# One 2 MB load of expert weights is issued ahead of a wait for the sorted token rows

## The chip, the cores and the metric

The kernel runs on one core of a Trainium2 chip. The metric is the device time of one execution in microseconds (us). PE is TensorE, DVE is VectorE, ACT is ScalarE, POOL is GpSimd, SP is SyncE; SP computes nothing and issues nearly all transfers between HBM and on-chip memory.

## The reference

Three layers over 512 tokens of width 1024. The first is a hybrid layer (latent attention and an RWKV-7 scan) that ends in a mixture of 32 experts; two layers with three mixing branches and a dense feed-forward follow. The change lies in the mixture of experts:

```python
expert_ids = gsel[:, None] * EXPERTS_PER_GROUP + top_idx      # two experts for each token
...
for e in range(N_EXPERTS):
    hidden = jax.nn.silu(t @ w_gate[e]) * (t @ w_up[e])       # 1024 -> 256
    y = y + combine[:, e:e + 1] * (hidden @ w_down[e])        # 256 -> 1024
```

Each expert has a gate and an up matrix (1 MB each in fp32) and a down matrix (1 MB).

## The kernel before

The program is one instruction stream per engine, written out by hand; the engines meet at semaphores. Its sections are A (the first layer's mixing and the routing), M (the experts), B (the last experts' results) and L (the other two layers). SP's stream is in `sp_all`, PE's share of section M in `pe_M`.

**Sorting.** Each token goes to two experts, and each expert has 64 row places. POOL writes the normalized rows of the tokens to their places in the HBM tensor `sorted_x` (in `pool_all`): first eight small indirect transfers of weights to `sorted_w` (L1575), then eight indirect transfers of 128 rows of 4 KB each (L1582, 512 KB each), which raise the semaphore `sorted`. These go through DMA queue q0; everything that SP issues goes through q1, and what ACT issues through q10.

**Pairs.** Section M handles the experts two at a time: 16 pairs, p = 0 to 15. For each pair PE does in this order:

- the gate and up products `gu{p}` (L1461, 32 matmuls). They need the pair's rows, already turned, and its gate and up weights, 4 MB in two transfers (x = 0 and 1, one expert each);
- the turning of the next pair's rows, `xt{0,1}_{p}` (`turn_rows`, L699, 8 transposes). They need the next pair's 128 rows in on-chip memory (`rows_in1`, `rows_in0`);
- the turning of the hidden values (L1474), the down products `md{0,1}_{p}` (L1493, 16 matmuls), and the products that put the pair before back into token order (L1441, L1442).

PE takes its instructions strictly in this order. Pair 0 needs no sorted row from HBM: its rows come from matmuls with a placement matrix (`px0`, `px1`, L687). The rows of pairs 1 and 2 are loaded from `sorted_x` by the loop over b (L2542), those of the later pairs by L2551.

**Weights.** `fill_gates(j, p)` (L2494) issues the two gate and up transfers of pair p into buffer j = p % 2, 2048 KB each. That buffer is free when `gu{p-2}` is done. One transfer is left out there: the first half of pair 2's gate weights goes to the idle `ring` instead (L2536). So `fill_gates(0, 2)` issues one transfer, the second half. `fill_down(p)` (L2500) issues the down weights, 1024 KB for each x, and `fill_down(1)` only one of them. Both are waited for on PE by `gates_full` and `down_full`.

SP goes through its list in order: a wait holds up all that stands behind it, and its transfers share one queue.

Of the kernel before, what the change touches and what calls it, by code (L numbers as in the profile page):

```python
# [21 lines left out]
P = 128  # L22
T = 512
NT = T // P
# [188 lines left out]
def build(nc, ts_, out):  # L213
# [40 lines left out]
    with ExitStack() as ctx:  # L254
# [3 lines left out]
        def sem(name):  # L258
            return ctx.enter_context(nc.semaphore(name))
# [27 lines left out]
        sorted_x = nc.dram_tensor("sorted_x", [ROWS + 2 * T, D], F32, kind="Internal").ap()  # L287
# [17 lines left out]
        def ev(name):  # L305
            if name not in events:
                events[name] = sem(name)
            return events[name]
# [995 lines left out]
        XG = [arena[:, 12800:12800 + D], arena[:, 15872:15872 + D]]  # L1304
# [1173 lines left out]
        def sp_all(sp):  # L2478
            e = sp.e
# [10 lines left out]
            def fill_gates(j, at_):  # L2490

                for x in range(2):
                    if (at_, x) != (2, 0):
                        e.dma_start(GATE_SLOTS[j][:, 4 * x:4 * x + 4, :], expert_slots(at_, 6 * x, 4)).then_inc(gates_full[j][x], 16)  # L2494

            def fill_down(at_):

                for x in range(2):
                    if (at_, x) != (1, 0):
                        e.dma_start(DOWN[:, 2 * x:2 * x + 2, :], expert_slots(at_, 6 * x + 4, 2)).then_inc(down_full[x], 16)  # L2500

            def expert_slots(at_, s, n):
                if isinstance(at_, int):
                    at_ = at0["M"] + at_ * RM + s
                    return stream[at_:at_ + n].rearrange("a p n -> p a n")
                return stream[bass.ds(at_ * RM + (at0["M"] + s), n)].rearrange("a p n -> p a n")
# [29 lines left out]
            e.dma_start(ring[:, 0:4, :], expert_slots(2, 0, 4)).then_inc(ev("ring_gates"), 16)  # L2536
            e.wait_ge(ev("weights_sorted"), 16 * 2 * NT)
            e.dma_start(ROW_WEIGHT, sorted_w[0:ROWS, :].rearrange("(n p) w -> p (n w)", p=P), allow_slow_non_contiguous=True).then_inc(ev("weights_in"), 16)
            e.wait_ge(ev("sorted"), 16 * 2 * NT)
            sp.e.wait_ge(*sp.filled("px1"))  # L2540
            for b in (1, 2):
                e.dma_start(XG[b % 2], sorted_x[b * P:(b + 1) * P, :]).then_inc(ev(f"rows_in{b % 2}"), 16)  # L2542
            sp.sec = "M"
            for p in range(NPAIR - 1):
                j = p % 2
                sp.e.wait_ge(*sp.filled(f"gu{p}"))
                if p < NPAIR - 2:
                    fill_gates(j, p + 2)
                if p < NPAIR - 3:
                    sp.e.wait_ge(*sp.filled(f"xt1_{p}"))  # L2550
                    e.dma_start(XG[1 - j], sorted_x[(p + 3) * P:(p + 4) * P, :]).then_inc(ev(f"rows_in{1 - j}"), 16)  # L2551
                sp.e.wait_ge(*sp.filled(f"md1_{p}"))
                fill_down(p + 1)
# [25 lines left out]
        @block.sync  # L2579
        def _(eng):  # L2580
            sp = Engine(eng, "sp")
            sp_all(sp)
# [210 lines left out]
```

## Time and profile before

| | |
|---|---|
| median of 3 runs | 2498.12 us (2497.9 to 2500.25) |
| the profiled execution | 2503.14 us, of which the span is 2501.3 us |
| PE busy | 2349.0 us (94%) |
| DVE busy | 1236.5 us (49%) |
| ACT busy | 748.0 us (30%) |
| POOL busy | 646.4 us (26%) |
| q1, SP's transfers | 278.51 MB |
| q0, POOL's transfers | 4.20 MB |
| chain that ended last | PE 78%, DVE 9%, DMA 7%, issue 3% |

The span is the time between the first and the last instruction of the profiled execution. Times inside it are counted from its start. The chain that ended last is followed back from the last instruction, at each step to what released it; its shares say where the time went. The digits of the page's slices are tenths: 9 is 90% busy or more.

### The profile page before, as it was taken

How to read it: one execution, taken by the hardware profiler on the slowest of the kernel's cores; microseconds unless marked ns; L12 is line 12 of the kernel's file. 1: busy time of each engine (PE TensorE's matmuls, PEld its weight loads, DVE VectorE, ACT ScalarE, POOL GpSimd, SP SyncE). 2: the span in 40 equal slices, each digit the busy share in tenths (PEclk: the TensorE clock that was granted, in tenths of full speed). 3: DMA queues.
4: the chain of work that ended last, by engine and by line, in shares of the span. 5: the costliest groups of instructions: out<-in, count | busy, mean ns of one | idle time of the engine just before them, and what ended most of it. 6: DMA issues, size and time to landing. Idle time of an engine off the chain costs nothing.

```text
span 2501.3 us, 30836 instructions
## 1 busy us (share of the span) xinstructions
PE 2349.0 (94%) x12552; PEld 1666.0 (67%) x12552; DVE 1236.5 (49%) x2171; ACT 748.0 (30%) x1176; POOL 646.4 (26%) x288
## 2 busy tenths in 40 slices
PE   6999778888899979999999999999999999999999
PEld 2334455563444448767878888888766887888887
DVE  2355555543365550585355677411177436666710
ACT  2333412212111123543233333223344323333321
POOL 0000000001000014223444444444322444444443
PEclk9999888879999989999999999999999999999999
DMA  5331000005899933212333333222211333333322
GB/s 200 109 93 34 30 2 2 2 5 227 335 409 409 402 126 110 68 51 77 96 97 94 94 100 94 92 93 104 86 60 51 100 94 93 96 98 96 98 76 101
DMA packets 79250, 287.79 MB, mean 115 GB/s; under 512 B 9187, under 2 KB 9571, under 8 KB 78598
## 3 DMA queue, kind: packets, MB, share of 16 engines
q1 hardware_dynamic: 75718, 278.51, 32.6%
q0 software_dynamic: 1408, 4.20, 0.4%
q10 hardware_dynamic: 1984, 3.10, 0.4%
q8 instruction: 101, 1.65, 0.3%
q14 instruction: 39, 0.32, 0.0%
HBM read 278.11 MB, written 16.07 MB: 118 GB/s over the span
## 4 chain that ended last, share of the span: by engine, by line
PE 78%; DVE 9%; DMA 7%; issue 3%; ACT 2%; POOL 1%; SPq 0%; ACTq 0%; DVEq 0%; another core or an unknown queue 0%; POOLq 0%
PE bank L1863 12%; PE bank L1865 12%; PE bank L1864 12%; DMA arena<-in_stream 6%; PE bank L530 5%; DVE arena L389 3%; PE bank L2012 3%; PE bank L2013 3%; PE bank L2011 3%; PE bank L1493 2%; PE bank L850 2%; PE bank L1848 2%; PE bank L1850 2%; PE bank L1849 2%; DVE arena L395 2%
## 5 line engine op out<-in xcount | busy, mean ns | idle before, releaser
L1594 POOL TENSOR_TENSOR ring_low<-ring,W_high 128x1024 fp32r<-128x1024 f32 x252 | 606.2, 2405 | 1135.4 <-ACT W_high L399 1135.4
L1863 PE MATMUL bank<-H_high,W_high 128*128 128x512 f32 x1408 | 555.4, 394 | 7.9 <-ACT arena L399 5.9
L1865 PE MATMUL bank<-H_high,ring_low 128*128 128x512 f32 x1408 | 548.4, 390 | 0.0
L1864 PE MATMUL bank<-H_low,W_high 128*128 128x512 f32 x1408 | 548.1, 389 | 0.0
L399 ACT ACTIVATE W_high<-ring 128x1024 fp32r<-128x1024 f32 x264 | 279.8, 1060 | 874.1 <-PE bank L1865 552.2
L1863 PEld LDWEIGHTS bank<-H_high,W_high 128*128 128x128 f32 x1408 | 264.2, 188 | 78.2 <-issue 23.2
L1864 PEld LDWEIGHTS bank<-H_low,W_high 128*128 128x128 f32 x1408 | 264.4, 188 | 55.8 <-issue 1.9
L1865 PEld LDWEIGHTS bank<-H_high,ring_low 128*128 128x128 f32 x1408 | 264.3, 188 | 55.6
L389 DVE TENSOR_TENSOR arena<-bank,root 128x512 f32<-128x512 f32 x116 | 79.7, 688 | 306.7 <-PE bank L1865 306.5
L399 ACT ACTIVATE arena<-bank 128x512 f32<-128x512 f32 (+5 forms) x179 | 77.0, 441 | 337.3 <-PE bank L825 118.0
L395 DVE SCALAR_TENSOR_TENSOR arena<-arena 128x512 f32<-128x512 f32 (+3 forms) x63 | 117.8, 1871 | 99.4 <-ACT arena L403 98.7
L1575 POOL DMA_INDIRECT sorted_w<-arena x8 | 7.8, 980 | 614.9 <-DVE arena L395 612.8
L389 DVE TENSOR_TENSOR arena<-arena 128x512 f32<-128x512 f32 (+5 forms) x180 | 146.8, 820 | 15.1 <-ACT arena L403 11.8
L2012 PE MATMUL bank<-arena_split,W_high 128*128 128x512 f32 x352 | 138.7, 394 | 0.0
L2011 PE MATMUL bank<-arena_split,W_high 128*128 128x512 f32 x352 | 137.5, 391 | 0.1
L2013 PE MATMUL bank<-arena_split,ring_low 128*128 128x512 f32 x352 | 137.5, 391 | 0.0
L530 PE MATMUL bank<-H,ring 128*128 128x512 f32 (+1 forms) x288 | 132.8, 606 | 2.3 <-DVE H L395 2.3
L395 DVE SCALAR_TENSOR_TENSOR arena<-arena,bank 64x64 f32<-64x64 f32 (+2 forms) x112 | 52.8, 474 | 165.3 <-ACT arena L403 101.1
L403 ACT ACTIVATE arena<-arena 128x512 f32<-128x512 f32 (+3 forms) x182 | 109.9, 620 | 72.8 <-DVE arena L1079 37.8
L395 DVE SCALAR_TENSOR_TENSOR X<-bank,X 128x512 f32<-128x512 f32 x32 | 22.1, 692 | 218.8 <-PE bank L2013 204.2
L395 DVE SCALAR_TENSOR_TENSOR arena<-arena,p 128x512 f32<-128x512 f32 x104 | 103.3, 993 | 40.8 <-ACT arena L403 39.0
L1461 PE MATMUL bank<-arena,early 128*64 128x512 f32 x496 | 113.0, 592 | 1.1 <-issue 1.1
(260 smaller groups left out, 3259.9 us busy)
## 6 DMA issues: line engine op xcount, KB each, us to landing
ring<-in_stream SPq DMA_DIRECT2D x289, 512.0 KB, 3.6
arena<-in_stream SPq DMA_DIRECT2D x31, 2048.0 KB, 12.8
arena<-in_stream SPq DMA_DIRECT2D x31, 1024.0 KB, 10.5
sorted_x<-in_zero_row SPq DMA_DIRECT2D x4, 2048.0 KB
arena<-sorted_x SPq DMA_DIRECT2D x15, 512.0 KB, 16.3
X<-in_x SPq DMA_DIRECT2D x1, 2048.0 KB, 9.0
ring<-in_stream SPq DMA_DIRECT2D x1, 2048.0 KB, 7.7
out<-X SPq DMA_DIRECT2D x8, 256.0 KB, 6.9
```

The source lines that it names most:

```text
L389: return V.tensor_tensor(o, a, b, op)
L395: return V.scalar_tensor_tensor(out=o, in0=a, scalar=s, in1=b, op0=op0, op1=op1)
L399: return S.activation(o, i, f)
L530: i = mm(o, w[:, k, 0:32] if m == 3 else w[:, k, :], H[:, k, :], start=k == 0, stop=k == KD - 1)
L1461: i = mm(o, XF[:, c, 64 * x:64 * x + 64], w, start=c == 0, stop=c == KD - 1)
L1594: return G.tensor_tensor(ring_low[:, slot, :], ring[:, slot, :], W_high[:, s % 2, :].bitcast(F32), ALU.subtract)
L1863: mm(ps[:, :], wh[:, k, :], H_high[:, k, :], start=k == 0, stop=False)
L1864: mm(ps[:, :], wh[:, k, :], H_low[:, k, :], start=False, stop=False)
L1865: i = mm(ps[:, :], wl[:, k, :], H_high[:, k, :], start=False, stop=k == KD - 1)
L2011: mm(ps[:, :], wh[:, t_ % TPS, :], high, start=k == 0, stop=False)
L2012: mm(ps[:, :], wh[:, t_ % TPS, :], low, start=False, stop=False)
L2013: i = mm(ps[:, :], wl[:, t_ % TPS, :], high, start=False, stop=k == KF - 1)
```

## The change

The loads of the rows of pairs 1 and 2, with the wait for `sorted` ahead of them, move into the first turn of the pair loop, behind `fill_gates(0, 2)`.

```diff
             e.wait_ge(ev("weights_sorted"), 16 * 2 * NT)
             e.dma_start(ROW_WEIGHT, sorted_w[0:ROWS, :].rearrange("(n p) w -> p (n w)", p=P), allow_slow_non_contiguous=True).then_inc(ev("weights_in"), 16)
-            e.wait_ge(ev("sorted"), 16 * 2 * NT)
             sp.e.wait_ge(*sp.filled("px1"))
-            for b in (1, 2):
-                e.dma_start(XG[b % 2], sorted_x[b * P:(b + 1) * P, :]).then_inc(ev(f"rows_in{b % 2}"), 16)
             sp.sec = "M"
             for p in range(NPAIR - 1):
                 j = p % 2
                 sp.e.wait_ge(*sp.filled(f"gu{p}"))
                 if p < NPAIR - 2:
                     fill_gates(j, p + 2)
+                if p == 0:
+                    e.wait_ge(ev("sorted"), 16 * 2 * NT)
+                    for b in (1, 2):
+                        e.dma_start(XG[b % 2], sorted_x[b * P:(b + 1) * P, :]).then_inc(ev(f"rows_in{b % 2}"), 16)
                 if p < NPAIR - 3:
                     sp.e.wait_ge(*sp.filled(f"xt1_{p}"))
```

On SP, between the last load of section A and the first turns of the pair loop, the difference is the following. L2536 is the first half of pair 2's gate weights, L2538 the weights of the sorted rows, L2494 a gate transfer (4x1024 elements on 128 partitions), `arena<-sorted_x` the rows of a pair, L2500 a down transfer. `bank_full0` is the semaphore of `px1` and of `gu0`.

```order
 L2536 DMA ring<-in_stream 128x4x1024 [waits bank_full2]
 L2538 DMA small<-sorted_w 128x16x1 [waits weights_sorted]
-L2542 DMA arena<-sorted_x 128x1024 [waits bank_full0,sorted]
-L2542 DMA arena<-sorted_x 128x1024
 L2494 DMA arena<-in_stream 128x4x1024 [waits bank_full0]
-L2551 DMA arena<-sorted_x 128x1024 [waits bank_full5]
+L2549 DMA arena<-sorted_x 128x1024 [waits sorted]
+L2549 DMA arena<-sorted_x 128x1024
+L2552 DMA arena<-sorted_x 128x1024 [waits bank_full5]
 L2500 DMA arena<-in_stream 128x2x1024 [waits bank_full0]
 L2494 DMA arena<-in_stream 128x4x1024 [waits bank_full1]
```

The two row loads moved behind one gate transfer; L2551 only has a new line number. No other engine's list differs except in line numbers.

## Rows read from the trace of the kernel before

**Rows 1.** The page: the span, and the DMA engines' busy tenths in 40 slices.
```profile
span 2501.3 us, 30836 instructions
...
DMA  5331000005899933212333333222211333333322
```

**Rows 2.** Timeline of SP, 605 to 720 us: start, length, line, operation.
```profile
624.38 0.37 SPq L2538 DMA_DIRECT2D small<-sorted_w  x1
637.27 0.81 SPq L2542 DMA_DIRECT2D arena<-sorted_x  x2
638.12 0.43 SPq L2494 DMA_DIRECT2D arena<-in_stream  x1
...
649.71 0.38 SPq L2500 DMA_DIRECT2D arena<-in_stream  x1
656.58 0.93 SPq L2494 DMA_DIRECT2D arena<-in_stream  x2
```

**Rows 3.** SP's own waits, 590 to 680 us: total, times, longest.
```profile
SPq L2542 <- DMA sorted_x<-arena: 12.4, 1, 12.4
```

**Rows 4.** Timeline of POOL: the first and the last of eight row scatters.
```profile
623.48 0.96 POOL L1582 DMA_INDIRECT sorted_x<-arena  x1 [0.31 <-issue]
...
632.29 0.95 POOL L1582 DMA_INDIRECT sorted_x<-arena  x1 [0.30 <-issue]
```

**Rows 5.** Timeline of PE, 610 to 705 us; in brackets the idle time before, and what ended it.
```profile
624.63 7.09 PE L1461 MATMUL bank<-arena,early 128*64 128x512 f32 x32 [1.10 <-issue]
...
641.24 1.97 PE L699 MATMUL bank<-cst,arena 128*128 128x128 f32 x8 [5.28 <-DMA arena<-sorted_x]
...
644.20 5.48 PE L1493 MATMUL bank<-arena 128*64 128x512 f32 x16 [0.56 <-ACT arena L399]
649.50 7.05 PE L1461 MATMUL bank<-arena,early 128*64 128x512 f32 x32
...
677.27 3.65 PE L1493 MATMUL bank<-arena 128*64 128x512 f32 x16
...
693.90 3.65 PE L1493 MATMUL bank<-arena 128*64 128x512 f32 x16 [0.95 <-DMA arena<-in_stream]
```

**Rows 6.** PE's waits from 660 to 880 us, the rest of section M.
```profile
PE bank L1493 <- DMA arena<-in_stream: 12.0, 12, 1.3
```

**Rows 7.** Busy time by stretch; PEclk is the granted clock, then DMA share, GB/s.
```profile
633.00:636.00 3.00, 1.37 (x10) 1.01 (x8) 0.00 (x0) 0.29 (x2) 0.24 (x1) 1.00 1.00 392
...
638.00:640.00 2.00, 0.00 (x0) 0.00 (x0) 0.00 (x0) 0.00 (x0) 0.00 (x0) 0.50 0.70 182
...
643.00:648.00 5.00, 4.43 (x13) 1.61 (x14) 3.21 (x6) 0.38 (x1) 0.00 (x0) 0.51 1.02 410
648.00:651.00 3.00, 3.00 (x16) 1.08 (x14) 1.34 (x2) 1.19 (x2) 0.00 (x0) 1.00 0.09 15
...
654.00:657.00 3.00, 3.00 (x17) 1.14 (x14) 0.00 (x0) 0.38 (x1) 0.00 (x0) 1.00 0.01 3
...
659.00:690.00 31.00, 31.00 (x148) 14.23 (x147) 18.57 (x33) 3.68 (x9) 0.00 (x0) 1.00 1.02 409
```

**Rows 8.** Issue to landing of the two row loads at L2542: min/median/max.
```profile
DMA to landing us min/median/max: 3.9/4.4/4.8
```

**Rows 9.** Issue to landing of L2494's three transfers between 630 and 660 us.
```profile
DMA to landing us min/median/max: 8.0/9.4/13.6
```

**Rows 10.** Timeline of ACT: the first operation on `gu0` and on `gu1`.
```profile
635.71 0.38 ACT L403 ACTIVATE arena<-bank 128x256 f32<-128x256 f32 x1 [10.79 <-remote]
...
656.59 0.38 ACT L403 ACTIVATE arena<-bank 128x256 f32<-128x256 f32 x1 [6.27 <-PE bank L1461]
```

**Rows 11.** DMA queues, 633 to 638 us: packets, MB, share of 16 engines.
```profile
q0 software_dynamic: 381, 1.36, 69.5%
```

**Rows 12.** DMA queues, 627 to 628 us.
```profile
q1 hardware_dynamic: 1217, 0.00, 68.4%
q0 software_dynamic: 63, 0.26, 62.6%
```

## Prediction

> **What bounds the kernel now.** I began with the page. The kernel spans 2501.3 us, and its DMA row has one stretch of nines, the slices from about 625 us on [rows 1]: the experts' weights. So I read that stretch engine by engine, SP first, since the change is only in SP's list.
>
> SP issues the load of the rows' weights at 624.38, then nothing until 637.27, when it loads the rows of pairs 1 and 2; right behind, at 638.12, comes pair 2's gate transfer [rows 2]. SP's own waits name the cause: 12.4 us for the scatter into `sorted_x` [rows 3]. POOL issues eight of these scatters between 623.48 and 632.29 [rows 4], and they keep the DMA engines full (share 1.00, 392 GB/s from 633 to 636 [rows 7]).
>
> Who needs what SP holds back? PE finishes `gu0` about 631.7 (624.63 + 7.09) and then idles until the rows of pair 1 are there: its transposes start at 641.24 after a wait for that very load [rows 5]. The rows were issued at 637.27 and took 3.9 us [rows 8], which is the 641.2. So the path is scatter, row load, transposes, and then PE in unbroken order: down products at 644.20, `gu1` at 649.50 [rows 5]. The end of `gu1` releases SP at 656.58 [rows 2] for pair 3's gate weights. From 659 on the DMA engines are full (share 1.02, 409 GB/s [rows 7]), and PE waits for down weights 12 times, 12.0 us in all, the first time at 693.90 [rows 5, 6]. The later pairs are therefore bound by a train of transfers whose first car leaves when `gu1` is done.
>
> **What the change does.** It adds no instruction and no byte. It moves two row loads behind one gate transfer of 2048 KB, 2.10 MB, on the same queue. There are two sides to cost.
>
> *The gate transfer comes earlier: worth nothing.* Its weights are wanted by `gu2`, which starts around 665 and shows no wait on it; PE's only waits after 660 are for down weights [rows 6]. Nor does it relieve the train. After it the queue runs dry: the DMA share is 0.09 from 648 to 651 and 0.01 from 654 to 657 [rows 7], so the train starts when `gu1` ends, not when the wires come free. The one down transfer between them is issued at 649.71 [rows 2], when PE is done with its buffer. The cover of this zero is those two dry stretches.
>
> *The rows come later: all of it on the path.* Two moments are unknown to the trace, since in it SP is held until 637.27: when SP would see `gu0`, and how q0 and q1 share the engines.
>
> The gate transfer's bytes need 2.10 MB / 409 GB/s = 5.1 us, a row load's 0.52 MB 1.3 us [rows 7].
>
> Early signal: the last `gu0` matmul ends at 631.7 and SP issues there; by the lag of a transfer into an idle queue (issue 656.58, DMA full by 659) its bytes run from about 633. The scatter then has 1.36 MB left [rows 11], 3.4 us at 392 to 409 GB/s. If the two queues share evenly, the scatter's tail takes twice as long, `sorted` comes 3.4 us late, the gate transfer is done a little after it, while the row load starts up, and the rows land 3.4 us late. If q1 goes first, the scatter stands still for the whole 5.1 us and the rows land 5.1 us late. The nearest row for that choice is the microsecond from 627 on, where SP's load of row weights meets the scatter: 1217 packets of q1 against 63 of q0 [rows 12]. Those packets are tiny, so it is weak evidence, but an even turn for turn it is not.
>
> Late signal: ACT, which waits for the same semaphore as SP would, starts on `gu0` only at 635.71, 4 us after the matmuls' end, with no local releaser named, while on `gu1` it starts at 656.59, at once [rows 10]. If SP sees it at 635.7 too, the scatter is nearly through and undisturbed, and SP is free again for its row loads at 637.27. The rows now stand in one queue behind the gate transfer. A gate transfer into an empty queue lands 8.0 us after issue [rows 9], so at 643.7; one row load behind it adds 1.3: 645.0, or 3.8 us late. Counted by bytes alone (wires free at about 636.6, then 5.1 + 1.3 us, then some 0.8 us until the landing is seen, an estimate from the rows of before, whose bytes and landing stand that far apart) it is 643.8, or 2.6 us late.
>
> So the path gets longer by 2.6 to 5.1 us. I take 4.2, the middle of the early signal's 3.4 and 5.1, with the late signal's 3.8 close by: I can't tell which signal holds in a run without the profiler.
>
> The Trainium skill (page "DMA: Bandwidth & Descriptors", section "Queues, rings and completion order") says that an engine consumes one row's descriptors in ring order and takes turns between rows packet by packet. Even turns would give the 3.4 us; the trace's microsecond from 627 doesn't look even and leans to 5.1. The ring order is what makes the late signal cost anything, and the trace agrees in that pair 2's gate transfer, behind two row loads, landed after 9.4 us where one into an empty queue took 8.0.
>
> *The clock.* PE sat idle before 641.24, and the granted clock was 0.50 from 638 to 640 and still 0.51 on average from 643 to 648, full after it [rows 7]. That is 1.2 instead of 2.4 GHz. The down products of pair 0 took 5.48 us because of it, against 3.65 for pair 2's [rows 5]. With a longer idle PE restarts at half clock as before. If the clock returned later, the whole group would run at half clock, 7.3 us (+1.8); if earlier, 3.65 (-1.8). I take nothing and keep 1.8 either way for the range, though less than the whole of it is likely.
>
> *The sum.* Removed: SP's 12.4 us hold on the gate transfer, worth 0. Added: 4.2 us ahead of pair 0's transposes. Moved through: `gu1`, the start of the train, everything behind it, one to one, since PE has no slack between 641.24 and 656.6 and the train none after. The profiled execution of 2503.14 us would become 2507.3; on the median of the runs, 5.0 lower, 2498.12 + 4.2 = 2502.3 us.
>
> **Rivals.**
>
> *No change.* The rows overtake the gate transfer, or the gate transfer's bytes run in the gaps: between 638 and 640 the DMA share was only 0.70 at 182 GB/s [rows 7]. If the two loads shared the wires evenly instead of in order, the rows would need 2 x 1.3 us, some 1.3 us more: 2499.4 us. Against it: the scatter leaves no gap before 636 (1.00). A change of the order that does nothing at all would need a signal from `gu0` later than 637.27, and ACT had it at 635.71. Chance 0.12.
>
> *Faster.* The early gate transfer takes its bytes out of the busy train, which ends up to 5.1 us sooner while the rows are delayed less than that; 2495 us at best. It decides if the queue is not empty when pair 3's gates are issued at 656.58. It was empty (0.01 from 654), so 0.03.
>
> *Worse than forecast.* q1 goes first, and the clock comes back late too: 5.1 + 1.8 = 6.9, 2505.0 us. The idle of PE grows from 5.28 to over 10 us, which speaks for it; that a restart cost the same 1.2 GHz already speaks against. Chance 0.12. The forecast, 3 to 5.1 us, keeps 0.73.
>
> **How the numbers follow.** A measurement of this kernel tells 0.2%, 5.0 us, from no change. Faster by that is left 0.03. The forecast straddles the bound only at its top: q1-first with 5.1 us stands on it. I give 0.23 of the forecast's 0.73 to the far side, with the worse rival's 0.12 that makes slower 0.35; the other 0.50 and the no-change rival's 0.12 make 0.62 for within 0.2%. The range takes in the 2.6 of the byte count less part of the clock's 1.8, and the upper 6.9 with a microsecond for the spread of the runs (2.35 us): 2498.8 to 2506.2 us.
>
> **What the next profile would show.** SP issues the 2048 KB transfer first, at 631.8 (early) or 635.7 (late), and the row loads behind it. Early, q0's share falls below 1.00 after 633 and SP sees `sorted` at 640.7 or, with q1 first, 642.4; late, at 637.3 as before, and the row loads' landing time grows from 3.9 to about 7.7 us. PE's idle before the transposes grows from 5.28 to about 9.5 us, and pair 3's gates go out at about 660.8 instead of 656.58. The waits for down weights stay near 12 us. I am wrong if the transposes start by 642, if the train starts by 657, or if what is lost there comes back in the later pairs.

## The result, and the profile after

The changed kernel takes 2507.06 us, the median of 8 runs (2503.48 to 2509.62), against 2498.01 us for the kernel before in its 8 (2496.93 to 2501.81). The ratio is 1.0029, with a 95% interval of 1.0019 to 1.0039: slower by some 7 us, between 4.7 and 9.7. (The two medians lie 9.1 us apart; that too is inside the interval.) That is beyond 0.2%, so of my three classes "slower" (0.35) came true and not the likeliest, "within 0.2%" (0.62). On the median of 2498.12 us the ratio gives 2505.4 us; I had said 2502.3, in a range of 2498.8 to 2506.2.

The page after, its span and its DMA row:

```profile
span 2506.9 us, 30836 instructions
...
DMA  5431000005899933212233233222221333333322
```

The two spans differ by 5.6 us (2506.9 against the 2501.3 of [rows 1]), but executions also differ in when they reach the stage at issue. I therefore count from one instruction that both have, the start of pair 0's row transposes (L699 on `early`), and call it S. It lies at 621.70 us after, and at 622.47 us before.

SP's timeline after, 605 to 720 us:

```profile
623.72 0.37 SPq L2538 DMA_DIRECT2D small<-sorted_w  x1
631.04 0.37 SPq L2494 DMA_DIRECT2D arena<-in_stream  x1
641.41 0.81 SPq L2549 DMA_DIRECT2D arena<-sorted_x  x2
...
653.11 0.38 SPq L2500 DMA_DIRECT2D arena<-in_stream  x1
659.98 0.93 SPq L2494 DMA_DIRECT2D arena<-in_stream  x2
```

The gate transfer goes out at 631.04, and the wait for `sorted` behind it ends at 641.41. From SP's load of the row weights that is 17.7 us; before it was 12.9 (637.27 - 624.38) [rows 2]. The scatter ends 4.8 us later. PE's and ACT's timelines after:

```profile
621.70 1.06 PE L699 MATMUL bank<-cst,early 128*128 128x128 f32 x8 [0.73 <-issue]
...
645.45 1.97 PE L699 MATMUL bank<-cst,arena 128*128 128x128 f32 x8 [12.16 <-DMA arena<-sorted_x]
...
648.41 4.67 PE L1493 MATMUL bank<-arena 128*64 128x512 f32 x16 [0.56 <-ACT arena L399]
652.90 7.05 PE L1461 MATMUL bank<-arena,early 128*64 128x512 f32 x32
...
697.54 3.65 PE L1493 MATMUL bank<-arena 128*64 128x512 f32 x16 [0.96 <-DMA arena<-in_stream]
```

```profile
631.00 0.38 ACT L403 ACTIVATE arena<-bank 128x256 f32<-128x256 f32 x1 [6.85 <-PE bank L1461]
```

PE starts pair 1's transposes 23.75 us after S, against 18.77 before [rows 5]: 5.0 us later. Its down products took 4.67 us against 5.48, so 0.8 us comes back, and pair 3's gates leave 38.28 us after S against 34.11 (656.58 - 622.47) [rows 2]: 4.2 us later. PE's waits for down weights hardly change, 11.5 us from 662 to 900 us against 12.0 before:

```profile
PE bank L1493 <- DMA arena<-in_stream: 11.5, 13, 1.1
```

Where did the scatter's 4.8 us go? The DMA queues of the kernel after, first 633 to 636 us, then 636 to 641 us:

```profile
q0 software_dynamic: 141, 0.49, 55.7%
q1 hardware_dynamic: 70, 0.29, 37.8%
q10 hardware_dynamic: 27, 0.04, 5.5%
```

```profile
q1 hardware_dynamic: 347, 1.42, 70.6%
q0 software_dynamic: 176, 0.61, 30.1%
q10 hardware_dynamic: 21, 0.02, 1.4%
```

Between 633 and 641 q1 moved 1.71 MB of the gate transfer while the scatter moved 1.10 MB (0.49 + 0.61). Neither had the wires to itself: from 636 on q1 had 1.42 of 2.05 MB, seven tenths. And the wires moved less while the two met. The stretches 634 to 636 and 636 to 638 us, whose last three numbers are clock, DMA share and GB/s:

```profile
634.00:636.00 2.00, 0.00 (x0) 0.00 (x0) 0.00 (x0) 0.00 (x0) 0.00 (x0) 1.00 0.94 266
636.00:638.00 2.00, 0.00 (x0) 0.00 (x0) 0.00 (x0) 0.00 (x0) 0.00 (x0) 0.71 1.02 402
```

That is 266 GB/s at a share of 0.94, where the scatter alone moved 392 at 1.00 [rows 7]. The loss is short: from 636 on the two move 402 together, as much as either alone.

That explains 4.2 us. But the end of the span lies 1885.2 us after S (2506.9 - 621.7) and before it was 1878.8 (2501.3 - 622.47): 6.4 us. The other 2.2 us are lost much later. PE in the first of the two last layers, the kernel after:

```profile
1091.68 0.49 PE L1919 MATMUL bank<-arena 64*128 64x128 f32 x4 [1.04 <-ACT arena L399]
1093.00 0.47 PE L1863 MATMUL bank<-H_high,W_high 128*128 128x512 f32 x1 [0.83 <-DVE arena L2306]
```

These two short waits are in the kernel before as well, ending at 1090.22. Now the 10 us from 2 us ahead of the second wait's end, first before, then after (PE's busy time, then clock, DMA share, GB/s):

```profile
1088.22:1098.22 10.00, 8.49 (x41) 1.00 0.12 47
```

```profile
1091.00:1101.00 10.00, 8.49 (x32) 0.83 0.12 49
```

The same place in the program, the same busy time, but in the kernel after the granted clock averages 0.83: for about a third of the time PE had 1.2 instead of 2.4 GHz, and it did 32 matmuls where it had done 41. The same happens one layer on, near 1882 us, at the same instructions, in the kernel after alone (again PE's busy time, clock, DMA share, GB/s):

```profile
1882.00:1886.00 4.00, 3.70 (x10) 0.59 0.00 0
```

So the loss has two parts, 4.2 us ahead of the train of transfers, and two stretches of half clock far behind it, 1.4 us each by this account (2.8 in all, of which 0.6 is made up for by the shift shrinking from 4.2 to 3.6 us on its way to the first of them).

### The profile page after: what moved, and what is told of

It is laid out like the page before. It is cut to its first block, busy times and chain, and to the rows that moved or that the text cites. A ratio compares the mean times of both kernels' runs of the same rounds, so it can differ in the third digit from the quotient of the medians.

```text
span 2506.9 us, 30836 instructions
## 1 busy us (share of the span) xinstructions
PE 2349.7 (94%) x12552; PEld 1668.8 (67%) x12552; DVE 1237.6 (49%) x2171; ACT 748.1 (30%) x1176; POOL 646.4 (26%) x288
## 4 chain that ended last, share of the span: by engine, by line
PE 78%; DVE 9%; DMA 7%; issue 3%; ACT 2%; POOL 1%; SPq 0%; ACTq 0%; DVEq 0%; another core or an unknown queue 0%; POOLq 0%
PE bank L1863 12%; PE bank L1865 12%; PE bank L1864 12%; DMA arena<-in_stream 6%; PE bank L530 5%; PE bank L2012 3%; PE bank L2013 3%; PE bank L2011 3%; DVE arena L389 3%; PE bank L1493 2%; PE bank L850 2%; PE bank L1848 2%; PE bank L1850 2%; PE bank L1849 2%; DVE arena L395 2%
## 5 line engine op out<-in xcount | busy, mean ns | idle before, releaser
L395 DVE SCALAR_TENSOR_TENSOR arena<-arena 128x512 f32<-128x512 f32 (+3 forms) x63 | 117.9, 1871 | 99.3 <-ACT arena L403 98.7
L395 DVE SCALAR_TENSOR_TENSOR arena<-arena,bank 64x64 f32<-64x64 f32 (+2 forms) x112 | 52.8, 474 | 161.5 <-ACT arena L403 97.2
L395 DVE SCALAR_TENSOR_TENSOR X<-bank,X 128x512 f32<-128x512 f32 x32 | 22.1, 692 | 218.8 <-PE bank L2013 204.2
L395 DVE SCALAR_TENSOR_TENSOR arena<-arena,p 128x512 f32<-128x512 f32 x104 | 103.3, 994 | 40.8 <-ACT arena L403 39.0
```

Of the source, the lines that this page charges most:

```text
L395: return V.scalar_tensor_tensor(out=o, in0=a, scalar=s, in1=b, op0=op0, op1=op1)
```

## The experiments

All kernels compute the reference's output in full. Theory **T**: the gate transfer and the scatter's tail share the wires, so `sorted` comes late. **Q**: the rows are late because they stand behind the gate transfer in their queue. **C**: the rest is TensorE's clock, which falls or doesn't fall at those two gaps by the moment at which they come. **M**: the rest is lost within section M. The columns count from S, all from profiles: the start of pair 1's transposes, the issue of pair 3's gates, the end of PE's wait on L2306 (the gap), the end of the span; then the granted clock over 10 us around the gap.

| kernel | transposes | pair 3's gates | gap | end | clock | ratio |
|---|---|---|---|---|---|---|
| before | 18.77 | 34.11 | 467.75 | 1878.8 | 1.00 | |
| after | 23.75 | 38.28 | 471.30 | 1885.2 | 0.83 | 1.0029 |
| r0, after again | 24.12 | 38.48 | 471.58 | 1885.5 | 0.83 | 1.0025 [1.0016, 1.0034] |
| r1, half ahead | 22.07 | 37.46 | 471.03 | 1882.2 | 1.00 | 1.0018 [1.0009, 1.0027] |
| r2, behind the wait | 24.53 | 38.69 | 474.13 | 1885.2 | 1.00 | 1.0031 [1.0018, 1.0043] |
| r3, rows on ACT | 24.09 | 38.47 | 471.50 | 1885.3 | 0.83 | 1.0025 [1.0016, 1.0034] |
| r4, rows scattered first | 11.42 | 27.50 | 460.76 | 1871.9 | 1.00 | 0.9965 [0.9953, 0.9978] |
| r5, between the rows | 18.87 | 34.18 | 467.79 | 1878.8 | 1.00 | 0.9997 [0.9988, 1.0007] |
| r6, quarter | 20.35 | 34.92 | 468.00 | 1881.9 | 0.83 | 1.0013 [1.0003, 1.0022] |
| r7, before again | 18.98 | 34.20 | 467.79 | 1878.9 | 1.00 | 0.9999 [0.9989, 1.0008] |
| r8, 6 memsets | 18.37 | 32.22 | 467.48 | 1878.5 | 1.00 | one run |
| r9, 14 memsets | 18.60 | 34.03 | 467.74 | 1878.8 | 1.00 | one run |
| r10, 34 memsets | 18.63 | 33.98 | 470.72 | 1881.9 | 1.00 | one run |
| r11, 27 memsets | 18.98 | 34.18 | 470.06 | 1881.3 | 1.00 | one run |

**r0, the changed kernel again.**

> The changed kernel once more, unedited. The local measure in all these runs is the time from SP's load of the row weights (small<-sorted_w) to PE's first transpose of pair 1 (arena, after the wait on sorted_x): 16.86 us before, 21.73 us after. Theory T (the gate transfer's 2.10 MB and the tail of the scatter share the wires, so the signal sorted comes late): 21.7 us again, SP's row loads 4 to 5 us later than before. Theory C (whatever the change costs beyond about 4 us is the clock of TensorE, which falls for a short stretch in the last two layers when a 2 us gap of PE falls badly): runs at mean clock 0.969 take 2 to 3 us longer than runs at 0.971, and the profile has 0 to 3 such stretches after 1000 us, each worth about 1.3 us. Rival to C (the shift itself costs more later, in the experts' loop): all runs would be near 2507 whatever their clock. I expect 2502 to 2509 us, median near 2505.

Median 2507.32 us (2501.59 to 2509.41, 11 runs). The transposes came 22.17 us after SP's load of the row weights, close to the 21.7. The two stretches of half clock are there again. The runs whose mean clock was 0.969 took 4.5 us longer than those at 0.971 (2508.1 against 2503.6), more than the 2 to 3 expected. But mean clock doesn't tell the two stretches apart from what happens ahead of S: r3 has both at a mean of 0.971. Traces are kept of one execution of each kernel, so whether every run of the changed kernel has the stretches stays open.

**r1, half of the gate transfer ahead.** The other half goes behind the row loads, and PE's wait on `ring_gates` goes from 16 to 32 to match. On SP:

```diff
...
-                if p < NPAIR - 2:
-                    fill_gates(j, p + 2)
                 if p == 0:
+                    src = expert_slots(2, 6, 4)
+                    e.dma_start(GATE_SLOTS[0][:, 4:6, :], src[:, 0:2, :]).then_inc(ev("ring_gates"), 16)
                     e.wait_ge(ev("sorted"), 16 * 2 * NT)
...
+                    e.dma_start(GATE_SLOTS[0][:, 6:8, :], src[:, 2:4, :]).then_inc(gates_full[0][1], 16)
+                elif p < NPAIR - 2:
+                    fill_gates(j, p + 2)
```

> Half of the gate transfer (1024 KB) ahead of the wait for sorted, the other half behind the two row loads. T: 1.05 MB ahead of the scatter's tail, 2.6 us at 409 GB/s, so the local measure is 19.2 to 19.5 us and the time about 2500.5 us. Rival Q (what counts is that the rows stand behind the gate transfer in SP's queue): a half transfer issued at about 631 has landed long before sorted is up, so nothing stands ahead of the rows any more: 16.9 to 17.3 us, 2498 us.

Median 2505.02 us. SP's timeline:

```profile
621.35 0.37 SPq L2538 DMA_DIRECT2D small<-sorted_w  x1
628.76 0.37 SPq L2546 DMA_DIRECT2D arena<-in_stream  x1
637.86 0.81 SPq L2549 DMA_DIRECT2D arena<-sorted_x  x2
```

`sorted` is seen 16.5 us after the load of the row weights, 3.6 us later than the 12.9 before. The half transfer was issued 9.1 us ahead of the row loads. It landed 9.2 us after its issue, just as they went out, not long before as expected, but they weren't held up: the transposes began 3.6 us behind their issue, 3.9 before. So Q, which expected 16.9 to 17.3 us from the load of the row weights to the transposes, is refuted as the cause here: they came at 20.15. T expected 19.2 to 19.5, by bytes alone. Half the bytes cost 3.1 to 3.3 us (against r7 and before) and all of them 4.8 to 5.4, so the price doesn't go by the size of the transfer. An estimate from rows fits both: the bytes of q1 that ran before the scatter was through, 1.04 MB here and 1.71 in the changed kernel, take 2.5 and 4.2 us at 409 GB/s, and the low rate where the queues meet (256 GB/s over 2 us here, 266 there, instead of some 400) costs some 0.7 us more: 3.2 and 4.9.

**r2, the gate transfer behind the wait, ahead of the rows.**

```diff
+                if p == 0:
+                    e.wait_ge(ev("sorted"), 16 * 2 * NT)
                 if p < NPAIR - 2:
                     fill_gates(j, p + 2)
                 if p == 0:
-                    e.wait_ge(ev("sorted"), 16 * 2 * NT)
                     for b in (1, 2):
```

> The gate transfer behind the wait for sorted, but still ahead of the two row loads. It cannot touch the scatter. T alone: no delay of sorted, SP sees it as before; if only the wires of the scatter mattered, the local measure is 16.9 us and the time 2498 us. Q: the rows wait for 2.10 MB in their own queue, 5.1 us: 21.5 to 22 us, 2502 to 2503 us. I expect Q to hold here, since a queue in order has to cost the same bytes wherever they stand ahead of the rows.

Median 2508.26 us. Here the scatter is left alone, and the gate transfer can only stand in the queue. SP, then PE:

```profile
636.80 0.37 SPq L2494 DMA_DIRECT2D arena<-in_stream  x1
637.22 0.98 SPq L2550 DMA_DIRECT2D arena<-sorted_x  x2
```

```profile
646.12 1.97 PE L699 MATMUL bank<-cst,arena 128*128 128x128 f32 x8 [12.95 <-DMA arena<-sorted_x]
```

The rows take 8.9 us from issue to use instead of 3.9 [rows 8], 5.0 us more, close to the 5.1 of 2.10 MB at 409 GB/s. From the load of the row weights the transposes come at 22.6 us, above the 21.5 to 22 expected; the rest is SP's own 0.4 us for issuing the gate transfer and some 0.4 us by which `sorted` comes later than in the trace of before (13.3 against 12.9, but 13.25 in r7). So Q is a real mechanism, with about the price of its bytes. It just isn't the one at work in the changed kernel, where the rows' own loads took the usual time (641.41 to 645.45, 4.0 us).

**r3, the row loads on ACT's queue.** The two loads and their wait move from SP to ACT, behind its first operation on `gu0`.

```diff
+                if p == 0:
+                    e.wait_ge(ev("sorted"), 16 * 2 * NT)
+                    for b in (1, 2):
+                        e.dma_start(XG[b % 2], sorted_x[b * P:(b + 1) * P, :]).then_inc(ev(f"rows_in{b % 2}"), 16)
                 if p == NPAIR - 2:
                     e.dma_start(RELB[0:32, 0, 0:DH], ts_["rel_bias"]).then_inc(ev("rel_in"), 16)
...
-                if p == 0:
-                    e.wait_ge(ev("sorted"), 16 * 2 * NT)
-                    for b in (1, 2):
-                        e.dma_start(XG[b % 2], sorted_x[b * P:(b + 1) * P, :]).then_inc(ev(f"rows_in{b % 2}"), 16)
```

> The gate transfer goes ahead as in the changed kernel, but the two row loads (and their wait for sorted) go to ACT's queue, so nothing of SP's stands ahead of them. T: sorted is as late as in the changed kernel, 4 to 5 us, and the rows are hardly sooner: 21 to 21.7 us, 2502 to 2505 us. Q: the rows are free of the gate transfer, 16.9 to 17.5 us, 2498 us.

Median 2505.71 us. ACT's queue carries nothing of the gate transfer, and ACT sees `sorted` no sooner:

```profile
638.94 0.84 ACTq L1519 DMA_DIRECT2D arena<-sorted_x  x2
```

That is 18.4 us after the load of the row weights (620.53), and the transposes follow 3.7 us later. T holds: the lateness is in the scatter, whatever queue the rows take.

**r5, the gate transfer between the two row loads.** Against the kernel before:

```diff
-            for b in (1, 2):
+            for b in (1,):
                 e.dma_start(XG[b % 2], sorted_x[b * P:(b + 1) * P, :]).then_inc(ev(f"rows_in{b % 2}"), 16)
...
                     fill_gates(j, p + 2)
+                if p == 0:
+                    e.dma_start(XG[0], sorted_x[2 * P:3 * P, :]).then_inc(ev("rows_in0"), 16)
```

> The order before, except that the gate transfer goes between the row load of pair 1 and that of pair 2. Bytes ahead of pair 1's rows are what costs: none are ahead of them here, so PE's first transpose of pair 1 comes 16.9 us after SP's load of the row weights, as before, and the time is that of before (2498 to 2500 us). Rival: pair 2's rows, late by 5 us, hold up PE at the second turn; they are wanted at 656.5 and would be there by 650, so this should not be seen.

Median 2499.72 us, no difference. Pair 2's rows have the slack that pair 1's lack.

**r6, a quarter of the gate transfer behind the wait, ahead of the rows.** Against r1:

```diff
-                    e.dma_start(GATE_SLOTS[0][:, 4:6, :], src[:, 0:2, :]).then_inc(ev("ring_gates"), 16)
                     e.wait_ge(ev("sorted"), 16 * 2 * NT)
+                    e.dma_start(GATE_SLOTS[0][:, 4:5, :], src[:, 0:1, :]).then_inc(ev("ring_gates"), 16)
...
-                    e.dma_start(GATE_SLOTS[0][:, 6:8, :], src[:, 2:4, :]).then_inc(gates_full[0][1], 16)
+                    e.dma_start(GATE_SLOTS[0][:, 5:8, :], src[:, 1:4, :]).then_inc(gates_full[0][1], 16)
```

> Only a quarter of the gate transfer (512 KB) stands behind the wait for sorted and ahead of the row loads, the other 1536 KB behind them. With the queue in order the rows are late by the bytes ahead of them: 0.52 MB at 409 GB/s, 1.3 us, so 18.2 us after SP's load of the row weights (16.9 with none, 22.6 with 2.10 MB), and pair 3's gate weights go out 1 to 1.3 us later than before. Rival (a fixed price for any transfer ahead, about 3 us, as the half transfer cost 3.3 us where its bytes account for 2.6): 20 us. The time would be 2499 to 2500 or 2501 to 2502 us.

Median 2503.05 us. The transposes came 18.46 us after the load of the row weights, 1.4 to 1.6 us later than before (16.86, 17.03), as 0.52 MB should cost; there is no fixed price. Part of it came back at once through the clock: pair 3's gates are 0.7 to 0.8 us late and the gap only 0.2. Yet the end is 3.0 us late, because both stretches of half clock are there. That is why the time, expected at 2499 to 2500 us, came out higher.

**r7, the kernel before again.**

> The kernel before, unedited, for its own spread: 16.9 us for the local measure again, 2498 to 2500 us, ratio 1.000. If ACT starts on gu0 at once here (not 4 us after the matmuls, as in the trace of before), that late signal was a singular event of one execution.

Median 2499.64 us. All its columns agree with before to 0.2 us. ACT starts on `gu0` at once:

```profile
630.84 0.38 ACT L403 ACTIVATE arena<-bank 128x256 f32<-128x256 f32 x1 [6.84 <-PE bank L1461]
```

**r4, rows scattered ahead of the weights.** On POOL the eight blocks of rows go first; on SP the row loads go ahead of the load of the row weights.

```diff
-            po.e.wait_ge(*po.nth("weights", 1))
-            for n in range(2 * NT):
...
                     nc.gpsimd.indirect_dma_start(sorted_x, bass.IndirectOffsetOnAxis(ap=rows, axis=0), HT[:, i_, :], None).then_inc(ev("sorted"), 16)
+            po.e.wait_ge(*po.nth("weights", 1))
+            for n in range(2 * NT):
...
```

> The order before on SP for the gate transfer, but POOL scatters the eight blocks of rows ahead of the eight small blocks of weights, and SP waits for the rows first. If the scatter's end is what everything behind hangs on, the rows of pair 1 are in place before gu0 ends, and the next thing late is the row weights: POOL is done with them 20 us after its start as before, about 633, their load of some 3.6 us is in by 638.2, so the turning of the hidden values (L1474), at 643.0 before, starts near 638.8: 4.2 us earlier, 2494 us. Rival (the freed time is lost again): the train of weight transfers, which starts when gu1 is done, would have to start no earlier than 656.6; then 2498 us. If the clock of TensorE is what makes up the rest, the time differs from the shift at 656 by 0 to 3 us.

Median 2490.94 us (2490.2 to 2494.74, 6 runs), ratio 0.9965: it beats both kernels, by some 9 and 16 us (7.0 and 13.3 from S to the end in the profiles). POOL's first scatter and PE:

```profile
605.47 1.15 POOL L1578 DMA_INDIRECT sorted_x<-arena  x1 [605.01 <-DVE arena L389]
```

```profile
628.65 1.04 PE L699 MATMUL bank<-cst,arena 128*128 128x128 f32 x8
631.62 0.41 PE L1474 MATMUL bank<-cst,arena 128*128 128x128 f32 x2 [1.94 <-DVE arena L395]
```

The transposes wait for nothing now; what is late next is the row weights, whose load DVE's L395 waits for (3.64 us) and PE behind it (1.94 us). Pair 3's gates go out 6.6 to 6.7 us earlier, not 4.2, because the rows need only the row numbers, not the weights, and POOL could start that much sooner: 11.8 us ahead of S (617.23 - 605.47), where the first scatter of weights in r7 started 9.3 us ahead of it (at 612.30, S at 621.55).

**r8 to r11, a pure delay on DVE.** In front of the signal that opens the last two layers, n memsets of one column:

```diff
+            for _ in range(n):
+                V.memset(small[:, 59:60], 0.0).then_inc(dv.chained(), 1)
+                dv.e.wait_ge(dv.chain, dv.n)
             V.memset(small[:, 59:60], 0.0).then_inc(dv.tells("x_ready"), 1)
```

> The kernel before with a pure delay: six tiny memsets of one unused column, one behind the other on DVE, ahead of the signal that opens the two last layers; section M is untouched. Measured from the start of pair 0's row transposes to the end of the span, before took 1878.8 us in both of its profiles, the changed kernel 1885.2 and 1885.5, of which 4.2 and 4.4 are there when pair 3's gate weights go out. Theory C (the other 2.2 us are two short stretches of half clock, near 1092 and 1880 us, that come or go with the moment at which the same 2 us gap of PE falls, whatever moved it): a delay of some 0.8 us may bring both stretches, as a shift of 0.8 us in r6 did: 0.8 + 2.2 = 3.0, 1881.8 us, with the granted clock of 1080:1110 at 0.94; if it brings none, 1879.6. Rival M (the 2.2 us come from something that the changed order does in the experts' section): never more than the delay itself, 1879.6, and no new stretch.

> The same with fourteen memsets, about 1.8 us. C: the gaps fall elsewhere again; either 1880.6 us with no new stretch or 1882.8 with two. M: 1880.6.

> The same with thirty-four memsets, about 4.2 us, the shift of the changed kernel. C: with the shift of 4.2 us the two stretches come back as in the changed kernel: 1878.8 + 4.2 + 2.2 = 1885.2 us and 0.94 in 1080:1110. M: 1883.0 us, 1.00 in 1080:1110.

> Twenty-seven memsets, about 3.35 us on DVE. The three delays before showed that some 2.6 us of this delay is hidden (1.69 us of memsets: 1878.8 us from the start of pair 0's transposes to the end, as before; 4.20 us: 1881.85, with one more stretch of half clock between 880 and 945), so this one should move PE in the last two layers by 0.8 to 1.2 us, the shift that r6 had. C: the gaps near 1088 and 1877 then fall where they fell in r6, two stretches of half clock come, the granted clock of 1080:1110 is 0.94, and the time is 1878.8 + 1 + 2.2 = 1882 us. M (the 2.2 us belong to the order of the transfers in section M): 1.00 in 1080:1110, 1879.6 to 1880 us. If the shift comes out above 1.5 us, it tells nothing new.

These tests did not decide. On DVE the memsets took 0.69, 1.69, 4.20 and 3.31 us (r8, r9, r10, r11). They also weren't pure delays: in r8, r10 and r11 the clock from 880 to 945 us averaged 0.84, where before and r9 have 0.87, one more stretch of half clock ahead of the gap. In r8, which was 1.9 us early at pair 3's gates and 0.3 at the gap, it cost 1.6 us. If it cost the same in the others, some 2.6 to 2.8 us of the delay is hidden. r8 and r9 hardly moved the gap (0.3 us early and not at all). r10 and r11 moved it by 3.0 and 2.3 us and brought no stretch near it. C had forecast stretches for both (1885.2 and 1882 us), but for shifts of 4.2 and of 0.8 to 1.2 us that didn't come about, and r11's is above the 1.5 us named ahead of the run as telling nothing; M's 1883.0 for r10 failed as well. The shift of 0.2 to 0.3 or of 3.5 to 3.8 us, at which the stretches came elsewhere, was not met.

What the table shows on C, over all kernels: relative to before, the end is as late as the gap, to 0.1 us, in every kernel whose clock there is 1.00 (among them r1 3.3 and 3.3; r10 3.0 and 3.0; r11 2.3 and 2.4; r4 -7.0 and -7.0). In the four with 0.83 the end is 2.7 to 2.8 us later than the gap: after (3.55 and 6.4), r0 (3.83 and 6.6), r3 (3.75 and 6.5), r6 (0.25 and 3.0). r2's gap was 6.4 us late, and so was its end; of those, 4.6 were there at pair 3's gates, and in the stretch 880 to 945 us its mean clock was 0.84 where before had 0.87, as in r8: it too lost to the clock, at another place. So M is refuted for after, r0, r3 and r6 (in the changed kernel 3.9 us are left at the end of section M, fewer than the 4.2 at pair 3's gates): what they lost beyond the gap they lost behind section M, at half clock. That the moment of the gap decides is what the table suggests (0.04 and 3.28 without, 0.25 and 3.55 with a stretch). So does the moment of the fall: in after, r0 and r3 it lies at 472.5 to 472.6 us behind S, though the gap ends anywhere from 471.30 to 471.58, and in r6 at 469.2, with the gap at 468.00. In each of the four it is 1.0 to 1.2 us behind the gap. None of this was forced by an experiment, so it stays an inference.

## Why the prediction was right in its direction and too small

**What bounds the stage.** Right: the path is scatter, row load, transposes, and all behind them. r4 is the strongest evidence: with the rows' scatter and row loads first in their queues, the kernel gained 7.0 us from S to the end. None of the three signs that the prediction named for being wrong came up: the transposes didn't start by 642, nor the train by 657, and little came back in the later pairs: at the last issue of down weights (L2500 at 867.63, before at 864.53) 3.9 of the 4.2 us are left.

**The earlier gate transfer is worth nothing.** Right. The wires are dry again ahead of the train (0 GB/s from 658 to 660, pair 3's gates at 659.98), and PE's waits for down weights stay at 11.5 to 11.8 us in every kernel with a changed place of the transfer.

**Early or late signal.** It was early: issue at 631.04. The late signal of the trace before [rows 10] is something that some executions have and others don't, 4 of the 14 profiles here (before, r8, r9, r10, each with 10.7 to 10.9 us of ACT's idle ended by no local releaser, against 6.8 elsewhere). It costs nothing there, as the rows come later still. My term for it, 3.8 us, was not needed. PE's idle ahead of the transposes, 12.16 us here, is to be compared with the 7.40 of r7, whose signal was early too, and not with the 5.28 of [rows 5].

**The size of the row delay.** 5.0 us at the transposes, and the term said 3.4 to 5.1, with 4.2 taken. The even share (3.4) was wrong, q1 first (5.1) nearly right in sum, but neither in mechanism: q1 had seven tenths of the bytes from 636 on, and the first meeting of the queues lost throughput. The transfer's bytes began late, too: 2.6 us after issue (631.04; q1 has no packet from 633.2 to 633.6 and nine in the 0.4 us behind), where I had counted some 1.3. The Trainium skill (page "DMA: Bandwidth & Descriptors", section "Queues, rings and completion order") has the engines take turns between queue rows packet by packet. Between 636 and 641 us the trace has 347 packets of q1 against 176 of q0, two for one, so turns are taken, but not evenly.

**The clock at the restart.** I took 0, within 1.8 either way. It gave back 0.8 us (4.67 against 5.48 us), so the train starts 4.2 us late. That is the sum that I had named, but by luck: as 5.0 - 0.8 and not as 4.2 + 0. Nor does this term belong to the order of the transfers alone: in r8, whose section M is that of the kernel before, the same down products took 3.99 us.

**"Moved through, one to one".** This is the step that failed. It held as far as the gap (3.6 us late), but not to the end. Behind PE's short waits at 1093 and 1882 us the clock fell to half, twice, 1.4 us each; that the shift brought this about, by changing the moment at which these waits fall, is inferred from the table. I had no term for a clock change outside the stage. With it the sum is 4.2 - 0.6 + 2.8 = 6.4 us, the profiles' difference from S on, and near the 7.2 us of the ratio (0.0029 x 2498). The 0.6 is what the shift loses between pair 3's gates and the gap (4.17 to 3.55).

**The rivals.** "Worse than forecast" came nearest in size (6.9 us), by luck too: its clock came back late at the restart, while the measured one came back early there and fell far behind it. "No change" and "faster" are out: the rows overtook nothing, and the queue was dry.

## What to carry to other kernels

An early transfer isn't free because its queue is idle. Before moving one forward, ask what else is on the wires then, on any queue, and whether the critical path waits for that; here 2.10 MB that nobody needed for over 30 us delayed a scatter that all waited for. What helped was to start the scatter's critical part first (r4), not to reorder around it. And when two kernels differ by less than 0.3%, compare where they stand at a few fixed instructions and look at the granted clock between them, before giving the whole difference to the edit.

## What the hardware showed that I had not expected

- A gap of 1.04 and one of 0.83 us, half a microsecond of work apart, cost PE half its clock for a stretch in 4 profiles and nothing in 10 others, though PE did the same there. The Trainium skill (page "TensorE: Matmul & The Clock Gate", Part 1) says that the gate's watch runs free and doesn't restart with the kernel, so that the point of a transition varies from run to run. Here the outcome went with the kernel: the changed kernel had both stretches in both of its profiles, and the kernel before had none in either. And the point didn't vary when it is counted from S: the first fall behind S came 15.1 to 15.3 us after it in all 14 profiles.
- Executions of one program reach S at different times, 616.4 to 622.5 us over these profiles, though the code ahead of it is the same in nearly all of them. From S on, the kernel before repeats to 0.02 us (1878.83 and 1878.85). In the first 600 us the granted clock averaged 0.91 in the execution that reached S last (before) and 0.92 in the one that reached it first (r9). So most of the 4 to 8 us spread of each kernel's runs can come from ahead of the stage at issue, and a count from a common instruction tells apart what the medians can't.
- A scatter and a load that meet on the wires moved 266 GB/s together over the first 2 us (264 in r0, 256 in r1), where either alone moves 390 to 410, and 402 in the 2 us behind. Why the start is slow isn't shown.
